# Shorter candidate lists, a fourth weight split for GpSimd, and VectorE's splits moved ahead in the choice of experts

## The chip, the cores and the metric

One core of a Trainium2 chip runs the whole program: TensorE (PE), VectorE (DVE), ScalarE (ACT), GpSimd (POOL) and the queue engine SyncE (SP), each with its own instruction stream, joined by semaphores. The metric is the device time of one execution in microseconds.

## The reference, cut to what matters

A two-layer model with a product-key mixture of experts ("PEER") in each layer, and a further block after it, on 256 tokens of width 1024, all in float32. In each layer the choice of experts is this:

```python
s1, i1 = lax.top_k(sc[:, :, 0], 16)      # sc: [256 tokens, 8 heads, 2, 128 keys]
s2, i2 = lax.top_k(sc[:, :, 1], 16)
cand = (s1[..., :, None] + s2[..., None, :])   # 16 x 16 pairs
cidx = i1[..., :, None] * 128 + i2[..., None, :]
top_s, pos = lax.top_k(cand, 16)
eidx = take_along_axis(cidx, pos)
gate = softmax(top_s)
```

After it every token's output is the sum over its 8 x 16 chosen experts of gate * gelu(x . u[e]) * v[e]. The kernel does not gather: it computes x . u for all 16384 experts, in 128 chunks of 128, and multiplies with a dense matrix of coefficients that is zero where an expert wasn't chosen.

## The kernel before, in words

**Weights.** Every weight block is a slot of 128 x 1024 float32 numbers. Slots pass through a ring of four buffers. SyncE loads slot n into `ring` once the low part of slot n-4 is made; ScalarE writes the rounded high part `ring_hi` (line 524, `split_hi`) once TensorE has used slot n-4; then VectorE or GpSimd subtracts to make the low part `ring_lo` (line 530, `split_lo`). Both engines use the same instruction with two tensors as inputs. One semaphore, `lo_ready`, counts the low parts in order of slots, so whoever makes the low part of slot n first waits until all earlier ones are there. TensorE multiplies each block in three products (lines 536 to 538: high x high, low x high, high x low), 24 matmuls a block.

**Who splits.** `POOL_SLOTS` lists the slots that GpSimd splits; VectorE takes all others, at places that are written out by hand. u0 is the first slot of the stage "expert.0" of a layer, in which TensorE multiplies 24 expert chunks while VectorE makes the choice. I call slot u0 + k **block k**. In the kernel before GpSimd splits the last query slots up to block 2, then blocks 4, 5, 6 and 14, 15, 16.

**The choice (`choose`, lines 1857 to 1938).** VectorE first finds the top 16 of the keys for each head (eight searches of 128 numbers for four rows each), then for each half t of the tokens (128 tokens, t = 0 and 1): converts the indices (L1874), builds the candidate sums (two TENSOR_TENSOR, L1882), searches the list of each head for its top 16 (`top16`, L1841 to L1854: maxima, their places, replacement, maxima, places), takes differences for the softmax (L1893, L1895), works out the two ranks of each winner from its place (L1898 to L1910), and looks up both indices (for x = 0 and 1: comparison L1915, product L1920, four sums L1926 and L1928), and scales the gates (L1934 to L1938, `picks_ready`). The sorted order of s1 and s2 means that pair (i, j) can only be among the top 16 if (i+1)(j+1) <= 16, so a list needs only some of the 256 pairs: before, 4 rows of 16 and 12 rows of 4, which is 112. Between these steps stand the calls `weights(n)`, each a split of one slot; `left` is the list of slots that is used up by the later calls.

**What follows.** TensorE transposes the picks (`turn_picks`, L922) between blocks 22 and 23; that needs `picks_ready` of both halves. ScalarE copies them out, VectorE builds one-hot matrices from them (L1977 to L1986), and TensorE multiplies these into coefficients in the next stage (L893), where another 24 expert chunks are interleaved. ScalarE's own order in expert.0 is: high part of block j+2, then the gelu of chunk j (L1332), and the softmax's exponentials (L1316) after chunks 7 and 19.

Of the kernel before, what the change touches and what calls it, by code (L numbers as in the profile page):

```python
# [16 lines left out]
ALU = mybir.AluOpType  # L17
# [25 lines left out]
PH = 8  # L43
TOPK = 16
GATE_SCALE = 2.0 ** 15
CANDS = 4 * TOPK + 4 * (TOPK - 4)
CHUNKS = NKEYS
FF = 2816
FC = FF // P
# [183 lines left out]
SLOTS, SLOT0 = plan_slots()  # L233

POOL_SLOTS = []
for _l in range(2):
    _u = SLOT0[f"expert{_l}.0"]
    POOL_SLOTS += [range(SLOT0[f"query{_l}"] + 5, _u + 3), range(_u + 4, _u + 7), range(_u + 14, _u + 17)]

# [23 lines left out]
def build(nc, a):  # L265
    with ExitStack() as ctx:
# [3 lines left out]
        def sem(name):  # L270
            return ctx.enter_context(nc.semaphore(name))
# [18 lines left out]
        rows = desk[:, :].bitcast(F16).rearrange("p (b n) -> p b n", b=3)  # L290
# [40 lines left out]
        def view(group, shape, arena=arena):  # L331

            n = int(np.prod(shape))
            at = used.get(group, 0)
            used[group] = at + n
            assert used[group] <= ARENA, group
            v = arena[:, at:at + n]
            names = "abcd"[:len(shape)]
            if len(shape) > 1:
                v = v.rearrange(f"p ({' '.join(names)}) -> p {' '.join(names)}",  # L340
                                **{x: s for x, s in zip(names[1:], shape[1:])})
            return v
# [27 lines left out]
        query = view("peer", [16, S])  # L370
# [11 lines left out]
        pair_ab = cand2.rearrange("p h n -> p (h n)")[:, 0:4 * PH * TOPK].rearrange("p (x k) -> p x k", x=4)  # L382
        pair_f = view("peer", [4 * PH * TOPK // 2]).bitcast(F16).rearrange("p (x n) -> p x n", x=4)
# [92 lines left out]
        vec = Tally(sem("vec_step"))  # L476
# [5 lines left out]
        def freed(w):  # L482
            return bank_free[w % 4], w // 4 + 1
# [1135 lines left out]
        def _(dve):  # L1619
            def step():  # L1620

                dve.wait_ge(vec.sem, vec.n)
# [234 lines left out]
            def choose(l):  # L1857
                u0 = SLOT0[f"expert{l}.0"]

                def weights(n):  # L1860

                    if any(n - 1 in r for r in POOL_SLOTS):
                        dve.wait_ge(lo_ready, n)
                    split_lo(dve, n)

                u32 = lambda v: v.bitcast(U32)
                for g in range(PH):
                    for t in range(NT):
                        dve.wait_ge(*freed(W0[f"query{l}"] + QUERY_ITEMS.index(("score", (t, g)))))
                    top16(lambda r: best[:, r // 2, 2 * g + r % 2, :], lambda r: u32(best_at[:, r // 2, 2 * g + r % 2, :]),  # L1870
                          lambda r: sub[:, g, r // 2, r % 2, :], lambda r: sub2[:, r // 2, r % 2, :], 4).then_inc(vec.sem, vec.up())
                    step()
                for t in range(NT):
                    dve.tensor_copy(best_f[:, t, :, :, :], u32(best_at[:, t, :, :]).rearrange("p (h x) r -> p x r h", x=2)).then_inc(vec.sem, vec.up())  # L1874

                    hp = best[:, t, :, :].rearrange("p (h x) k -> p h x k", x=2)
                    for lo, i0, rows, width in ((0, 0, 4, TOPK), (4 * TOPK, 4, TOPK - 4, 4)):
                        part = cand[:, :, lo:lo + rows * width].rearrange("p h (i j) -> p h i j", j=width)  # L1880
                        part_shape = [P, PH, rows, width]
                        dve.tensor_tensor(part, hp[:, :, 0, i0:i0 + rows].unsqueeze(3).to_broadcast(part_shape),  # L1882
                                          hp[:, :, 1, 0:width].unsqueeze(2).to_broadcast(part_shape), ALU.add).then_inc(vec.sem, vec.up())
                    shape = [P, PH, TOPK, TOPK]
                    step()
                    weights(u0 + (3, 13)[t])
                    left = iter(range(u0 + (7, 17)[t], u0 + (13, 24)[t]))
                    top = pair[:, t, :].rearrange("p (h k) -> p h k", k=TOPK)
                    at = pair_at.rearrange("p (h k) -> p h k", k=TOPK)
                    top16(lambda r: top[:, r, :], lambda r: u32(at[:, r, :]), lambda r: cand[:, r, 0:CANDS], lambda r: cand2[:, r, 0:CANDS], PH).then_inc(vec.sem, vec.up())  # L1890
                    step()

                    dve.tensor_copy(psum8[:, t, 1, :], top[:, :, 0]).then_inc(vec.sem, vec.up())  # L1893
                    step()
                    dve.tensor_tensor(top, top, psum8[:, t, 1, :].unsqueeze(2).to_broadcast([P, PH, TOPK]), ALU.subtract).then_inc(gate_diff_ready, 1)  # L1895

                    for y, (op, amount) in enumerate(((ALU.logical_shift_right, 4), (ALU.bitwise_and, TOPK - 1), (ALU.logical_shift_right, 2), (ALU.bitwise_and, 3))):
                        dve.tensor_scalar(u32(pair_ab[:, y, :]), u32(pair_at), amount, None, op).then_inc(vec.sem, vec.up())  # L1898
                    step()
                    weights(next(left))  # L1900
                    dve.tensor_copy(pair_f.rearrange("p x (k h) -> p x k h", h=PH), u32(pair_ab[:, :, :]).rearrange("p x (h k) -> p x k h", h=PH)).then_inc(vec.sem, vec.up())
                    step()

                    dve.scalar_tensor_tensor(pair_ab[:, 0, :], pair_f[:, 2, :], 4.0 - TOPK, pair_f[:, 0, :], ALU.add, ALU.subtract).then_inc(vec.sem, vec.up())
                    dve.tensor_tensor(pair_ab[:, 1, :], pair_f[:, 3, :], pair_f[:, 1, :], ALU.subtract).then_inc(vec.sem, vec.up())
                    step()
                    for x in range(2):
                        dve.scalar_tensor_tensor(pair_ab[:, 2 + x, :], pair_f[:, 2, :], float(TOPK), pair_ab[:, x, :], ALU.is_ge, ALU.mult).then_inc(vec.sem, vec.up())
                    step()
                    dve.tensor_tensor(pair_f[:, 0:2, :], pair_f[:, 0:2, :], pair_ab[:, 2:4, :], ALU.add).then_inc(vec.sem, vec.up())  # L1910
                    step()
                    for x in range(2):

                        shape = [P, TOPK, PH * TOPK // 4, 4]
                        dve.tensor_tensor(rank_hot.rearrange("p r (n f) -> p r n f", f=4), pair_f[:, x, :].rearrange("p (n f) -> p n f", f=4).unsqueeze(1).to_broadcast(shape),  # L1915
                                          ranks[:, :, :].unsqueeze(2).to_broadcast(shape), ALU.is_equal).then_inc(vec.sem, vec.up())
                        step()
                        weights(next(left))
                        shape = [P, TOPK, TOPK, PH]
                        dve.tensor_tensor(rank_key.rearrange("p r (k h) -> p r k h", h=PH), rank_hot.rearrange("p r (k h) -> p r k h", h=PH),  # L1920
                                          best_f[:, t, x, :, :].unsqueeze(2).to_broadcast(shape), ALU.mult).then_inc(vec.sem, vec.up())
                        step()
                        weights(next(left))

                        for n in (8, 4, 2):
                            dve.tensor_tensor(rank_key[:, 0:n, :], rank_key[:, 0:n, :], rank_key[:, n:2 * n, :], ALU.add).then_inc(vec.sem, vec.up())  # L1926
                            step()
                        dve.tensor_tensor(chosen[:, t, x, :], rank_key[:, 0, :], rank_key[:, 1, :], ALU.add).then_inc(vec.sem, vec.up())  # L1928
                        step()
                        if t or not x:  # L1930
                            weights(next(left))
                    gate = chosen[:, t, 2, :].rearrange("p (k h) -> p h k", h=PH)
                    dve.wait_ge(gate_exp_ready, NT * l + t + 1)
                    dve.tensor_reduce(psum8[:, t, 0, :], gate, AX.X, ALU.add).then_inc(vec.sem, vec.up())  # L1934
                    step()
                    dve.reciprocal(psum8[:, t, 0, :], psum8[:, t, 0, :]).then_inc(vec.sem, vec.up())
                    step()
                    dve.tensor_tensor(gate, gate, psum8[:, t, 0, :].unsqueeze(2).to_broadcast([P, PH, TOPK]), ALU.mult).then_inc(picks_ready, 1)  # L1938
# [438 lines left out]
```

## Time and profile before

| what | value |
|---|---|
| median of 3 runs | 2502.95 us (2501.2 to 2504.99) |
| profiled execution | span 2499.7 us from its first to its last instruction; no other time is listed for it |
| median less that span | 3.25 us |
| granted TensorE clock | 0.999 of full speed |
| busy in the span | PE 98%, DVE 76%, ACT 50%, POOL 5% |
| expert.0 of layer 0 | 188.3 to 263.3 us |
| expert.0 of layer 1 | 1111.2 to 1186.2 us |

The span is what the trace shows of the execution; the median is over whole executions and holds 3.25 us more. The engines' shares are averages over the program; the two stages named in the last rows are where the change lies.

### The profile page before, as it was taken

To read this page: it belongs to the slowest core of one execution; us is meant where nothing else is said; L and a number is where in the kernel's file an instruction comes from. 1 tells how busy PE (TensorE), PEld (TensorE's weight loads), DVE (VectorE), ACT (ScalarE), POOL (GpSimd) and SP (SyncE) were. 2 spreads that over 40 slices of the span, in tenths; PEclk is the share of its full clock that TensorE was granted. 3 is DMA by queue.
4 is the path that set the end of the run, shared out by engine and by line. 5 is a ranking of instruction groups with operands and counts; after the bars stand their busy time and mean duration, and the time that the engine had idled before them with its cause. 6 is when DMAs were issued, how large, how long until landed. Compare 5 with 4: busy or idle time off the path is not lost.

```text
span 2499.7 us, 48393 instructions
## 1 busy us (share of the span) xinstructions
PE 2455.1 (98%) x17776; PEld 2276.9 (91%) x17776; DVE 1900.3 (76%) x3687; ACT 1255.6 (50%) x2085; POOL 132.3 (5%) x115
## 2 busy tenths in 40 slices
PE   9999999999999999999999999999999999999999
PEld 8998998999999888999988999999889999899999
DVE  6789997666666788889996666666886767787774
ACT  6754884444444334455874444444335445556443
POOL 0042000000000000051000000000000001100000
PEclk9999999999999999999999999999999999999999
DMA  7444677666655554545676666655554555524555
GB/s 241 143 156 172 188 210 240 205 214 210 210 194 189 188 186 168 186 145 193 189 216 227 210 210 210 208 195 186 187 190 137 175 185 175 139 95 152 178 183 163
DMA packets 192136, 465.70 MB, mean 186 GB/s; under 512 B 81546, under 2 KB 83722, under 8 KB 191088
## 3 DMA queue, kind: packets, MB, share of 16 engines
q1 hardware_dynamic: 118736, 419.99, 50.6%
q0 software_dynamic: 6624, 24.28, 3.3%
q10 hardware_dynamic: 66624, 19.40, 3.2%
q8 instruction: 95, 1.56, 0.2%
q14 instruction: 57, 0.47, 0.1%
HBM read 443.02 MB, written 20.59 MB: 185 GB/s over the span
## 4 chain that ended last, share of the span: by engine, by line
PE 50%; DVE 2%; ACT 1%; issue 0%; DVEq 0%; ACTq 0%
PE acc L879 14%; PE work L536 9%; PE work L537 9%; PE work L538 9%; PE acc L536 2%; PE acc L537 1%; PE acc L538 1%; PE work L893 1%; PE work L1107 1%; DVE ring_lo L530 1%; PE work L1093 0%; PE work L1080 0%; PE work L719 0%; PE work L718 0%; PE work L717 0%
## 5 line engine op out<-in xcount | busy, mean ns | idle before, releaser
L530 DVE TENSOR_TENSOR ring_lo<-ring,ring_hi 128x1024 fp32r<-128x1024 f32 x758 | 921.3, 1219 | 429.8 <-ACT ring_hi L524 428.1
L524 ACT ACTIVATE ring_hi<-ring 128x1024 fp32r<-128x1024 f32 (+1 forms) x798 | 832.6, 1050 | 442.7 <-PE acc L879 370.1
L536 PE MATMUL work<-normed_hi,ring_hi 128*128 128x256 f32 (+1 forms) x2512 | 714.0, 284 | 17.6 <-DVE ring_lo L530 11.6
L537 PE MATMUL work<-normed_lo,ring_hi 128*128 128x256 f32 (+1 forms) x2512 | 708.5, 282 | 0.0
L538 PE MATMUL work<-normed_hi,ring_lo 128*128 128x256 f32 (+1 forms) x2512 | 706.3, 281 | 0.0
L879 PE MATMUL acc<-ring_hi,weighed 128*128 128x512 f32 x2048 | 588.4, 396 | 4.8 <-DVE weighed L2010 4.8
L536 PEld LDWEIGHTS work<-normed_hi,ring_hi 128*128 128x128 f32 x2512 | 472.7, 188 | 31.3 <-DVE ring_lo L530 13.4
L537 PEld LDWEIGHTS work<-normed_lo,ring_hi 128*128 128x128 f32 x2512 | 473.6, 189 | 7.9
L538 PEld LDWEIGHTS work<-normed_hi,ring_lo 128*128 128x128 f32 x2512 | 472.1, 188 | 0.0
L879 PEld LDWEIGHTS acc<-ring_hi,weighed 128*128 128x128 f32 x2048 | 373.8, 188 | 83.9 <-DVE weighed L2010 5.2
L536 PE MATMUL work<-arena_parts,ring_hi 128*128 128x256 f32 (+1 forms) x1184 | 336.6, 284 | 3.6 <-DVE arena L2242 2.0
L538 PE MATMUL work<-arena_parts,ring_lo 128*128 128x256 f32 (+1 forms) x1184 | 334.0, 282 | 0.0
L537 PE MATMUL work<-arena_parts,ring_hi 128*128 128x256 f32 (+1 forms) x1184 | 333.6, 282 | 0.0
L879 PE MATMUL acc<-ring_lo,weighed 128*128 128x512 f32 x1024 | 323.0, 396 | 0.0
L1332 ACT ACTIVATE arena<-work 128x256 f32 (+1 forms) x192 | 73.8, 384 | 349.7 <-PE work L538 349.7
L879 PEld LDWEIGHTS acc<-ring_lo,weighed 128*128 128x128 f32 x1024 | 192.7, 188 | 45.6
L536 PEld LDWEIGHTS work<-arena_parts,ring_hi 128*128 128x128 f32 x1184 | 223.3, 189 | 4.5 <-DVE arena L2242 2.2
L537 PEld LDWEIGHTS work<-arena_parts,ring_hi 128*128 128x128 f32 x1184 | 223.3, 189 | 0.1
L538 PEld LDWEIGHTS work<-arena_parts,ring_lo 128*128 128x128 f32 x1184 | 223.1, 188 | 0.0
L2004 DVE TENSOR_TENSOR product<-arena 128x256 f32 (+1 forms) x256 | 157.0, 613 | 2.5 <-ACT arena L1346 2.5
L536 PE MATMUL acc<-normed_hi,ring_hi 128*128 128x256 f32 x512 | 154.5, 302 | 0.0
L537 PE MATMUL acc<-normed_lo,ring_hi 128*128 128x256 f32 x512 | 143.9, 281 | 0.0
(298 smaller groups left out, 2522.1 us busy)
## 6 DMA issues: line engine op xcount, KB each, us to landing
ring<-in_u SPq DMA_DIRECT2D x256, 512.0 KB, 3.3
ring<-in_v SPq DMA_DIRECT2D x256, 512.0 KB, 3.3
ring<-in_ffn_in SPq DMA_DIRECT2D x88, 512.0 KB, 3.3
ring<-in_query SPq DMA_DIRECT2D x32, 512.0 KB, 3.3
ficients_of_later_chunks<-gate_b ACTq DMA_DIRECT2D x32, 512.0 KB, 4.6
arena<-ficients_of_later_chunks POOLq DMA_DIRECT2D x32, 512.0 KB, 4.0
ring<-in_ffn_out SPq DMA_DIRECT2D x32, 512.0 KB, 4.1
ring<-in_even_in SPq DMA_DIRECT2D x27, 512.0 KB, 3.9
```

The costliest lines, as they stand in the source:

```text
L524: act.activation(ring_hi[:, n % RING, 0:width], ring[:, n % RING, 0:width], ACT.Copy).then_inc(hi_ready, 1)
L530: eng.tensor_tensor(ring_lo[:, n % RING, 0:width], ring[:, n % RING, 0:width], ring_hi[:, n % RING, 0:width].bitcast(F32), ALU.subtract).t ...
L536: pe.matmul(out, w_hi, hi, start=start, stop=False, **more)
L537: pe.matmul(out, w_hi, lo, start=False, stop=False, **more)
L538: return pe.matmul(out, w_lo, hi, start=False, stop=stop, **more)
L879: mm = pe.matmul(acc[:, 2 * half + t, :], tokens, rows[:, m, half * 512:(half + 1) * 512], start=(e == 0 and x == 0), stop=(e == CHUNKS - ...
L893: mm = pe.matmul(work[:, w % 4, t * P:(t + 1) * P], hot_second[b][:, t // 2, :, t % 2], hot_gated[b][:, x, t // 2, :, t % 2], start=(x == ...
L1107: mm = pe.matmul(work[:, w % 4, t * P:S], v, prob2[:, u % 2, b, t:NT, :].rearrange("p t q -> p (t q)"), start=(b == 0), stop=(b == NT), sk ...
L1332: act.activation(into, work[:, w % 4, 0:S], ACT.Gelu).then_inc(bank_free[w % 4], 1)
L2004: dve.tensor_tensor(product[:, e % 2, :], hid, co, ALU.mult).then_inc(coef_read, 1)
```

## The change

Three things change, in both layers. The candidate lists have 3 rows of 16 and 13 rows of 4 pairs, which is 100 in place of 112, and the constants that turn a place into ranks follow. GpSimd splits blocks 4 to 7 and 14 to 17. VectorE's own splits are placed anew: block 3 ahead of the index conversion and candidate sums of the first half; block 8 (18 in the second half) right behind the differences; blocks 9 to 13 (19 to 23) behind the comparisons, products and the first lookup's sums. The split of block 13 was the last thing before the second search, and is now inside the second lookup of the first half.

```diff
-CANDS = 4 * TOPK + 4 * (TOPK - 4)
+WIDE = 3
+CANDS = WIDE * TOPK + 4 * (TOPK - WIDE)
...
-    POOL_SLOTS += [range(SLOT0[f"query{_l}"] + 5, _u + 3), range(_u + 4, _u + 7), range(_u + 14, _u + 17)]
+    POOL_SLOTS += [range(SLOT0[f"query{_l}"] + 5, _u + 3), range(_u + 4, _u + 8), range(_u + 14, _u + 18)]
...
                     step()
+                weights(u0 + 3)
                 for t in range(NT):
                     dve.tensor_copy(best_f[:, t, :, :, :], ...)
...
-                    for lo, i0, rows, width in ((0, 0, 4, TOPK), (4 * TOPK, 4, TOPK - 4, 4)):
+                    for lo, i0, rows, width in ((0, 0, WIDE, TOPK), (WIDE * TOPK, WIDE, TOPK - WIDE, 4)):
...
                     step()
-                    weights(u0 + (3, 13)[t])
-                    left = iter(range(u0 + (7, 17)[t], u0 + (13, 24)[t]))
+                    left = iter(range(u0 + (8, 18)[t], u0 + (14, 24)[t]))
...
                     dve.tensor_tensor(top, top, psum8[:, t, 1, :]..., ALU.subtract).then_inc(gate_diff_ready, 1)
+                    weights(next(left))
 
                     for y, (op, amount) in enumerate(...):
                         dve.tensor_scalar(u32(pair_ab[:, y, :]), u32(pair_at), amount, None, op).then_inc(vec.sem, vec.up())
                     step()
-                    weights(next(left))
...
-                        if t or not x:
+                        if not x:
                             weights(next(left))
```

GpSimd's stream first: `ring_lo` rows are its splits, a row that waits for `lo_ready` waits for VectorE's split of the slot before. This is layer 0 before, from its first query slot to its first load of coefficients:

```order
L530 ISA
L530 TENSOR_TENSOR ring_lo<-ring,ring_hi 128x1024 [waits hi_ready,lo_ready]
L530 TENSOR_TENSOR ring_lo<-ring,ring_hi 128x1024 [waits hi_ready] x13
L530 TENSOR_TENSOR ring_lo<-ring,ring_hi 128x1024 [waits hi_ready,lo_ready]
L530 TENSOR_TENSOR ring_lo<-ring,ring_hi 128x1024 [waits hi_ready] x2
L530 TENSOR_TENSOR ring_lo<-ring,ring_hi 128x1024 [waits hi_ready,lo_ready]
L530 TENSOR_TENSOR ring_lo<-ring,ring_hi 128x1024 [waits hi_ready] x2
```

And the same place in the changed kernel, whose line numbers are higher by one:

```order
L531 ISA
L531 TENSOR_TENSOR ring_lo<-ring,ring_hi 128x1024 [waits hi_ready,lo_ready]
L531 TENSOR_TENSOR ring_lo<-ring,ring_hi 128x1024 [waits hi_ready] x13
L531 TENSOR_TENSOR ring_lo<-ring,ring_hi 128x1024 [waits hi_ready,lo_ready]
L531 TENSOR_TENSOR ring_lo<-ring,ring_hi 128x1024 [waits hi_ready] x3
L531 TENSOR_TENSOR ring_lo<-ring,ring_hi 128x1024 [waits hi_ready,lo_ready]
L531 TENSOR_TENSOR ring_lo<-ring,ring_hi 128x1024 [waits hi_ready] x3
```

Each of the two later groups has four splits in place of three. VectorE's stream before, at the start of the first half: the conversion, the candidate sums, the split of block 3 and the search.

```order
L1874 CAST arena<-arena 128x256
L1882 TENSOR_TENSOR arena<-arena 128x8x64
L1882 TENSOR_TENSOR arena<-arena 128x8x48
L530 TENSOR_TENSOR ring_lo<-ring,ring_hi 128x1024
L1841 MAX arena<-arena 128x8 x8
```

In the changed kernel the split of block 3 stands first, and it is what releases GpSimd for blocks 4 to 7:

```order
L531 TENSOR_TENSOR ring_lo<-ring,ring_hi 128x1024
L1876 CAST arena<-arena 128x256
L1884 TENSOR_TENSOR arena<-arena 128x8x48
L1884 TENSOR_TENSOR arena<-arena 128x8x52
L1842 MAX arena<-arena 128x8 x8
```

VectorE's stream before, from the last sums of the first half's second lookup to the second search:

```order
L1926 TENSOR_TENSOR arena<-arena 128x256
L1928 TENSOR_TENSOR arena<-arena 128x128
L1934 TENSOR_REDUCE arena<-arena 128x8
L1936 RECIPROCAL arena<-arena 128x8
L1938 TENSOR_TENSOR arena<-arena 128x8x16
L1874 CAST arena<-arena 128x256
L1882 TENSOR_TENSOR arena<-arena 128x8x64
L1882 TENSOR_TENSOR arena<-arena 128x8x48
L530 TENSOR_TENSOR ring_lo<-ring,ring_hi 128x1024
L1841 MAX arena<-arena 128x8 x8
```

In the changed kernel, the same stretch from block 13's split on:

```order
L531 TENSOR_TENSOR ring_lo<-ring,ring_hi 128x1024
L1927 TENSOR_TENSOR arena<-arena 128x1024
L1927 TENSOR_TENSOR arena<-arena 128x512
L1927 TENSOR_TENSOR arena<-arena 128x256
L1929 TENSOR_TENSOR arena<-arena 128x128
L1935 TENSOR_REDUCE arena<-arena 128x8
L1937 RECIPROCAL arena<-arena 128x8
L1939 TENSOR_TENSOR arena<-arena 128x8x16
L1876 CAST arena<-arena 128x256
L1884 TENSOR_TENSOR arena<-arena 128x8x48
L1884 TENSOR_TENSOR arena<-arena 128x8x52
L1842 MAX arena<-arena 128x8 x8
```

The split that releases GpSimd for blocks 14 to 17 has moved from just ahead of the search to ten other instructions earlier.

## Rows read from the trace of the kernel before

**Rows 1.** The page: the span, and busy time (share of the span) by engine.
```profile
span 2499.7 us, 48393 instructions
PE 2455.1 (98%) x17776; PEld 2276.9 (91%) x17776; DVE 1900.3 (76%) x3687; ACT 1255.6 (50%) x2085; POOL 132.3 (5%) x115
```

**Rows 2.** Waits in expert.0, layer 0 then 1: us in total, times, longest.
```profile
PE work L536 <- DVE ring_lo L530: 5.3, 4, 1.5
...
PE work L536 <- DVE ring_lo L530: 5.4, 4, 1.5
```

**Rows 3.** TensorE's timeline: start us, us, what, xcount [idle before <- releaser].
```profile
198.11 0.39 PE L536 MATMUL work<-normed_hi,ring_hi 128*128 128x256 f32 x1 [1.09 <-DVE ring_lo L530]
...
214.12 0.39 PE L536 MATMUL work<-normed_hi,ring_hi 128*128 128x256 f32 x1 [1.48 <-DVE ring_lo L530]
...
229.76 0.38 PE L536 MATMUL work<-normed_hi,ring_hi 128*128 128x256 f32 x1 [1.24 <-DVE ring_lo L530]
...
245.77 0.39 PE L536 MATMUL work<-normed_hi,ring_hi 128*128 128x256 f32 x1 [1.47 <-DVE ring_lo L530]
```

**Rows 4.** ScalarE's timeline: high part of block 5, gelu of chunks 4 and 5.
```profile
197.33 1.05 ACT L524 ACTIVATE ring_hi<-ring 128x1024 fp32r<-128x1024 f32 x1
...
204.07 0.39 ACT L1332 ACTIVATE gate_b<-work 128x256 f32<-128x256 f32 x1 [1.50 <-PE work L538]
...
206.89 0.38 ACT L1332 ACTIVATE gate_b<-work 128x256 f32<-128x256 f32 x1 [1.50 <-PE work L538]
```

**Rows 5.** VectorE over both halves: stretch and its length, busy; then its waits.
```profile
195.30:260.10 64.80, 62.77 (x204) 1.00 0.51 179
...
DVE ring_lo L530 <- ACT ring_hi L524: 0.3, 1, 0.3
```

**Rows 6.** Timeline, last instruction of the choice and TensorE's transposes of the picks.
```profile
259.74 0.42 DVE L1938 TENSOR_TENSOR arena<-arena 128x128 f32<-128x128 f32 x1
...
260.01 0.82 PE L922 MATMUL work<-const,arena 128*128 128x128 f32 x6
```

**Rows 7.** VectorE's timeline in the first half.
```profile
195.32 0.41 DVE L1874 CAST arena<-arena 128x256 f16<-128x256 uint32 x1
195.63 1.17 DVE L1882 TENSOR_TENSOR arena<-arena 128x512 f32<-128x512 f32 x2
196.83 1.23 DVE L530 TENSOR_TENSOR ring_lo<-ring,ring_hi 128x1024 fp32r<-128x1024 f32 x1
197.97 1.51 DVE L1841 MAX8 arena<-arena 128x8 f32<-128x112 f32 x8
...
199.59 0.27 DVE L1845 FIND_INDEX8 arena<-arena 128x8 uint32<-128x112 f32 x1
...
207.18 0.17 DVE L1893 COPY arena<-arena 128x8 f32<-128x8 f32 x1
...
208.26 1.23 DVE L530 TENSOR_TENSOR ring_lo<-ring,ring_hi 128x1024 fp32r<-128x1024 f32 x1
...
224.14 1.47 DVE L1926 TENSOR_TENSOR arena<-arena 128x1024 f16<-128x1024 f16 x3
...
225.98 0.43 DVE L1934 TENSOR_REDUCE arena<-arena 128x8 f32<-128x128 f32 x1
...
226.68 0.41 DVE L1938 TENSOR_TENSOR arena<-arena 128x128 f32<-128x128 f32 x1
```

**Rows 8.** Groups by form, lists of 128 and 112 numbers: busy us, mean ns.
```profile
L1854 DVE FIND_INDEX8 arena<-arena 128x8 uint32<-128x128 f32 x2 | 0.5, 285 | 0.0
...
L1854 DVE FIND_INDEX8 arena<-arena 128x8 uint32<-128x112 f32 x1 | 0.3, 268 | 0.0
```

**Rows 9.** GpSimd's splits: durations (ns min/median/max) of all 40, and its timeline.
```profile
L530 POOL TENSOR_TENSOR ring_lo<-ring,ring_hi x40: 2374/2397/2417, 147.5 to 1157.5; 128x1024 fp32r<-128x1024 f32 x40
...
198.13 7.11 POOL L530 TENSOR_TENSOR ring_lo<-ring,ring_hi 128x1024 fp32r<-128x1024 f32 x3 [5.68 <-DVE ring_lo L530]
229.79 7.12 POOL L530 TENSOR_TENSOR ring_lo<-ring,ring_hi 128x1024 fp32r<-128x1024 f32 x3 [24.54 <-DVE ring_lo L530]
```

More of the change, by code:

```diff
@@ L1899, in choose @@
                     step()
-                    weights(next(left))
                     dve.tensor_copy(pair_f.rearrange("p x (k h) -> p x k h", h=PH), u32(pair_ab[:, :, :]).rearrange("p x (h k) -> p x k h", h=PH)).then_inc(vec.sem, vec.up())
                     step()
-                    dve.scalar_tensor_tensor(pair_ab[:, 0, :], pair_f[:, 2, :], 4.0 - TOPK, pair_f[:, 0, :], ALU.add, ALU.subtract).then_inc(vec.sem, vec.up())
+                    dve.scalar_tensor_tensor(pair_ab[:, 0, :], pair_f[:, 2, :], WIDE - 4.0 * WIDE, pair_f[:, 0, :], ALU.add, ALU.subtract).then_inc(vec.sem, vec.up())
                     dve.tensor_tensor(pair_ab[:, 1, :], pair_f[:, 3, :], pair_f[:, 1, :], ALU.subtract).then_inc(vec.sem, vec.up())
@@ L1907, in choose @@
                     for x in range(2):
-                        dve.scalar_tensor_tensor(pair_ab[:, 2 + x, :], pair_f[:, 2, :], float(TOPK), pair_ab[:, x, :], ALU.is_ge, ALU.mult).then_inc(vec.sem, vec.up())
+                        dve.scalar_tensor_tensor(pair_ab[:, 2 + x, :], pair_f[:, 2, :], 4.0 * WIDE, pair_ab[:, x, :], ALU.is_ge, ALU.mult).then_inc(vec.sem, vec.up())
                     step()
```

## The prediction

> **What bounds the kernel now.** I read the page first: TensorE is busy 98% of the 2499.7 us, so time can only come from, or go to, the places where it waits [rows 1]. The waits of expert.0 name one cause, `ring_lo` from VectorE: 5.3 us in four waits in layer 0 and 5.4 us in four in layer 1 [rows 2]. The timeline places them: blocks 3, 8, 13 and 18 [rows 3]. TensorE takes 206.89 - 204.07 = 2.82 us a block [rows 4]; 24 blocks are 67.7 us, the stage lasts 75.0 and the transposes take some 0.6, so about 6.5 us a layer are really lost (the profile models the end of a matmul late, so it shows 5.3).
>
> VectorE makes most of those splits between the steps of the choice, and it is full: from 195.3 to 260.1 it waits once, 0.3 us [rows 5]. Its chain also sets the end of the stage. Its last instruction, L1938, runs 259.74 to 260.16, and TensorE starts the transposes of the picks at 260.01, first half first [rows 6]. So TensorE arrives there just when VectorE is done: **two chains end together**. Taking away TensorE's waits alone gives nothing; the stage ends earlier only by as much as VectorE's chain gets shorter, up to 6.5 us a layer.
>
> **The change, part by part, if VectorE and GpSimd run freely beside each other.**
> - Two splits a layer go to GpSimd (blocks 7 and 17). On VectorE a split costs the distance to the next instruction, 197.97 - 196.83 = 1.14 us [rows 7]: 2 x 1.14 = 2.28 us.
> - A list is 12 numbers shorter. A place search of 128 numbers took 285 ns and one of 112 took 268: 1.06 ns a number [rows 8], 12.8 ns an instruction. A half has 5 groups of 8 search instructions (two of maxima, two of places, one of replacement; the small value loads between them don't change): 40 x 12.8 = 0.51 us. The candidate sums have 96 numbers fewer, 0.10 us. Two halves: 1.22 us. The constants that turn a place into ranks cost nothing: same instructions, same sizes.
> - The 0.3 us wait of rows 5 was for ScalarE's high part of block 22. With an earlier TensorE it goes, against which VectorE may wait a little at blocks 8 and 10, where it is now earlier than ScalarE. I take 0.2 net.
> - Together 3.7 us of VectorE a layer. TensorE: block 3's wait goes, since its split stands 1.5 us earlier (195.32 instead of 196.83 [rows 7]); blocks 8 and 13 come in time. The other 2.8 us of its 6.5 it will still wait, at block 19 or for the picks. So it is VectorE's 3.7 us, not TensorE's 6.5, that the stage gains.
> - GpSimd's fourth split in each group is hidden by TensorE's pace: a split takes 2.40 us [rows 9], less than 2.82 a block, and ScalarE's high parts come one a block.
>
> Freely beside each other this gives 2502.95 - 2 x 3.7 = 2495.5.
>
> **What the new places bring together.** All 40 splits of GpSimd in the profile take 2.374 to 2.417 us, and every one lies beside a search or an idle VectorE; in expert.0 the groups start at 198.13 and 229.79, right behind VectorE's split of blocks 3 and 13, and end within the searches [rows 7, 9]. A search instruction reads one tensor. Beside GpSimd it costs nothing: 0.27 us at 199.59, as long as one without [rows 7, 8]. But a split on either engine reads two. There is **no row in which a two-tensor instruction of VectorE lies beside a split of GpSimd**, and the change makes many:
> - First half. Block 4 can start 0.07 us behind VectorE's block 3 (198.13 against 196.83 + 1.23 [rows 7, 9]), so at 196.6; the candidate sums would start at 195.32 + 1.14 + 0.31 = 196.8.
> - Between the halves. Block 13's split now stands inside the second lookup and releases blocks 14 to 17. Then come sums L1926 and L1928 (224.14 to 225.98: 1.8 us), the reduction and reciprocal (0.7 us, one tensor) and L1938 [rows 7], the conversion and candidate sums (1.5 us): 4.4 us, most of it two-tensor, ahead of the second search.
>
> The cost is bounded by nothing (above: 3.7 us gained), and by each engine waiting for the other's whole instruction. In that case, worked out on the first layer:
> - Candidate sums wait from 196.8 to 199.0 (2.2 us); if GpSimd's block 5 follows at once, whose high part is there at 198.4 [rows 4], to 201.4 (4.6 us).
> - Between the halves at least two splits get in: one at the reduction, so L1938 waits 2.4 - 0.7 = 1.7 us, the next ahead of the candidate sums, 2.2 us. At most VectorE stands behind three to four splits, 8.8 us: GpSimd's rows come merged in threes at 7.11 us, so its splits follow with no gap when the high parts are there [rows 9].
> - Sum: 6.1 to 13.4 us a layer, middle 9.8.
>
> VectorE's chain is then longer than before by 9.8 - 3.7 = 6.1 us a layer, TensorE waits for blocks 8 or 9 and for 18 and 19, and the picks come 6 us late. What stands behind the picks shifts by the same: VectorE builds one-hots from them without a break, and TensorE has no slack in 98% of the span. Two layers: +12.2, ends +4.8 and +19.4.
>
> The Trainium skill speaks against the change here: "SBUF — State Buffer", section "Who interferes with whom", says that a VectorE instruction with two inputs in SBUF and a GpSimd instruction that reads SBUF contend for a shared read interface, and that the second to start is blocked until the first has finished. By it the sum is the second one, 2515; by rows 9 alone, which show no such pair, both ends stay open.
>
> **Which end I take.** No row decides. The break-even does part of it: 3.7 us a layer is one and a half GpSimd splits, and at least four of the eight in a layer fall where VectorE wants two tensors. If a third of their 9.6 us is waited for, the gain is gone. Of all shares of waiting between none and all, most lie on the losing side. So I forecast **waiting: 2502.95 + 12 = 2515**, its own range 2505 to 2523.
>
> **Rivals.**
> - Free overlap: 2495.5. For it: nothing in the profile shows a cost of running both. Against it: nothing shows that pair. Chance 0.20. This is the one on the other side; it decides from less than 3.7 us of waiting a layer.
> - Short waiting: VectorE's three sums L1926 follow each other without a gap (1.47 us merged [rows 7]), so GpSimd may find a gap only at the reduction, and at block 4 it might come behind the candidate sums. Then 2 to 6 us a layer: -1.7 to +2.3, 2500 to 2508. Chance 0.22, two thirds of it within 0.2%.
> - GpSimd's own lateness: if its block 17 is not there when block 18 is due, VectorE stands (it waits for `lo_ready`). GpSimd needs 4 x 2.40 = 9.6 us and, at one high part per 2.82 us, spans some 11 us against a search of 8.7 (207.18 - 197.97 - 0.51 [rows 7]). That by itself costs little, since block 17 starts over 2 us before the search ends; only a delay by VectorE's instructions makes it matter. It lies inside the forecast.
> - The forecast, 6 to 13 us of waiting: 0.58.
>
> **The numbers.** A measurement of this kernel can tell about 0.2% (5 us) from no change. Slower by more: 0.58 less the part of it that just touches +4.8 (0.04), plus 0.06 of the short waiting, 0.60. Within 0.2%: 0.15 + 0.04, 0.19. Faster: 0.20 and 0.01, 0.21. The range must reach the free case, since that alone holds 2 in 10: 2495 to 2523.
>
> **What the new profile would show.** Right: VectorE's candidate sums of the first half begin late, by 2 us or more, with no semaphore as a cause, or last over 2 us; the same at L1939 (the old L1938) and the second candidate sums; splits longer than 2.42 us on GpSimd and 1.23 on VectorE; TensorE waits at blocks 8 or 9 and 18, 19; picks later than 260.2. Wrong: the candidate sums take 1.1 us together and start at once, the picks are done near 256.4, and TensorE waits only at block 19 and ahead of the transposes. A search must be shorter by 0.5 us in either case: that is a check on the 1.2 us of the lists. What would make the forecast wrong is a free pair; what would make it wrong in size is how the two engines take turns, on which I took the middle.

## The result, and the profile after

The changed kernel takes 2513.7 us (median of 4 runs, 2511.28 to 2518.85) against 2503.11 us for the kernel before, measured beside it (4 runs, 2501.2 to 2504.99): ratio 1.0048, interval 1.0036 to 1.006. It is slower by 10.6 us. The profiled execution has a span of 2509.7 us and a time of its own of 2511.63.

The page's first lines, which answer to [rows 1]:

```profile
span 2509.7 us, 48391 instructions
PE 2460.5 (98%) x17776; PEld 2281.7 (91%) x17776; DVE 1909.6 (76%) x3683; ACT 1255.8 (50%) x2085; POOL 144.4 (6%) x119
```

VectorE has two splits a layer less, 4 x 1.14 = 4.6 us, and shorter lists, and yet 9.3 us more busy time. That is the first sign: a wait for the other engine is counted as work. The rows to look at are VectorE's in the first half of layer 0 (timeline: start us, us, instruction, count, idle before):

```profile
195.18 1.23 DVE L531 TENSOR_TENSOR ring_lo<-ring,ring_hi 128x1024 fp32r<-128x1024 f32 x1
196.32 0.39 DVE L1876 CAST arena<-arena 128x256 f16<-128x256 uint32 x1
196.63 5.47 DVE L1884 TENSOR_TENSOR arena<-arena 128x384 f32<-128x384 f32 x2
202.13 1.41 DVE L1842 MAX8 arena<-arena 128x8 f32<-128x100 f32 x8
...
210.85 0.17 DVE L1894 COPY arena<-arena 128x8 f32<-128x8 f32 x1
```

and between the halves:

```profile
226.67 1.23 DVE L531 TENSOR_TENSOR ring_lo<-ring,ring_hi 128x1024 fp32r<-128x1024 f32 x1
227.81 1.47 DVE L1927 TENSOR_TENSOR arena<-arena 128x1024 f16<-128x1024 f16 x3
...
229.64 0.41 DVE L1935 TENSOR_REDUCE arena<-arena 128x8 f32<-128x128 f32 x1
230.09 0.20 DVE L1937 RECIPROCAL arena<-arena 128x8 f32<-128x8 f32 x1
230.33 1.86 DVE L1939 TENSOR_TENSOR arena<-arena 128x128 f32<-128x128 f32 x1
...
232.31 3.26 DVE L1884 TENSOR_TENSOR arena<-arena 128x384 f32<-128x384 f32 x2
```

GpSimd's splits over the same time:

```profile
196.48 10.24 POOL L531 TENSOR_TENSOR ring_lo<-ring,ring_hi 128x1024 fp32r<-128x1024 f32 x4 [4.19 <-DVE ring_lo L531]
229.50 2.41 POOL L531 TENSOR_TENSOR ring_lo<-ring,ring_hi 128x1024 fp32r<-128x1024 f32 x1 [22.78 <-ACT ring_hi L525]
232.24 2.41 POOL L531 TENSOR_TENSOR ring_lo<-ring,ring_hi 128x1024 fp32r<-128x1024 f32 x1 [0.33 <-ACT ring_hi L525]
235.04 5.21 POOL L531 TENSOR_TENSOR ring_lo<-ring,ring_hi 128x1024 fp32r<-128x1024 f32 x2 [0.39 <-ACT ring_hi L525]
```

Lay the two side by side. The split of 229.50 ends at 231.91; L1939, started at 230.33, ends 0.28 us after that, at 232.19. The split of 232.24 ends at 234.65; the two sums of L1884 end at 235.57. The reduction and the reciprocal in the same split's shadow keep their usual length [rows 7]. The timeline merges the sums of L1884; the groups by form take them apart, for 196.5 to 202.3 us (busy us, mean ns):

```profile
L1884 DVE TENSOR_TENSOR arena<-arena 128x416 f32<-128x416 f32 x1 | 2.8, 2782 | 0.0
L1884 DVE TENSOR_TENSOR arena<-arena 128x384 f32<-128x384 f32 x1 | 2.8, 2761 | 0.0
```

Each stood behind one split of 2.4 us, with 0.0 us of idle time and no releaser shown. GpSimd pays a little too: its four splits take 10.24 us here and 9.47 in a kernel in which no two-tensor instruction lies beside them (experiment 3).

TensorE waits at blocks 8 and 9, 18 and 19 and for the picks (timeline of layer 0; the first four rows answer to [rows 3], the last to [rows 6]):

```profile
212.54 0.39 PE L537 MATMUL work<-normed_hi,ring_hi 128*128 128x256 f32 x1 [1.49 <-DVE ring_lo L531]
...
217.78 0.39 PE L537 MATMUL work<-normed_hi,ring_hi 128*128 128x256 f32 x1 [2.16 <-DVE ring_lo L531]
...
246.02 0.39 PE L537 MATMUL work<-normed_hi,ring_hi 128*128 128x256 f32 x1 [1.23 <-DVE ring_lo L531]
...
251.28 0.38 PE L537 MATMUL work<-normed_hi,ring_hi 128*128 128x256 f32 x1 [2.17 <-DVE ring_lo L531]
...
264.42 0.52 PE L923 MATMUL work<-const,arena 128*128 128x128 f32 x3 [1.24 <-DVE arena L1939]
```

**Where the 10.0 us of the span went.** I measure the choice from its first instruction to the end of its last one. Before, 195.32 to 260.16: 64.84 us [rows 6, 7]. After, 195.18 to 264.27 (L1939 starts at 263.88 and takes 0.39): 69.09, and in layer 1 by the same reckoning 69.16 against 64.86. That is +4.25 and +4.30. The remaining 1.5 us lie between the two choices. Windows over the same 5792 matmuls, before and after (stretch and length; busy us of PE, PEld, DVE, ACT, POOL; granted clock; DMA share; GB/s), first the kernel before:

```profile
264.00:1111.20 847.20, 838.54 (x5792) 761.86 (x5791) 649.16 (x1190) 413.06 (x665) 40.56 (x31) 1.00 0.60 196
...
356.00:376.00 20.00, 17.53 (x156) 15.88 (x156) 18.25 (x34) 14.92 (x35) 0.00 (x0) 1.00 0.73 213
```

and the changed kernel:

```profile
268.00:1116.70 848.70, 840.14 (x5792) 763.48 (x5792) 649.40 (x1190) 413.13 (x664) 40.57 (x31) 1.00 0.61 196
...
360.00:380.00 20.00, 17.52 (x149) 15.76 (x149) 18.25 (x34) 13.82 (x34) 0.00 (x0) 0.91 0.77 215
```

The second pair is the place: the same busy time, seven matmuls fewer, and a granted clock of 0.91 where it was 1.00. A share of 0.91 over 20 us is some 3.5 us at the lower of TensorE's two levels (1.2 in place of 2.4 GHz), and costs half of that. The profile of experiment 6, whose granted clock between the choices is 1.00 as in the kernel before, has 858.4 us from the end of one choice to the start of the next (262.05 to 1120.49); the kernel before has 858.2 (260.16 to 1118.34), the changed kernel 859.6 (264.27 to 1123.87). So 8.5 us are what the two choices have become longer, and 1.5 us a dip of TensorE's clock 100 us later.

### The profile page after: what moved, and what is told of

Its sections match the earlier page's. It is cut to its first block, busy times and chain, and to the rows that moved or that the text cites. A ratio compares the mean times of both kernels' runs of the same rounds, so it can differ in the third digit from the quotient of the medians.

```text
span 2509.7 us, 48391 instructions
## 1 busy us (share of the span) xinstructions
PE 2460.5 (98%) x17776; PEld 2281.7 (91%) x17776; DVE 1909.6 (76%) x3683; ACT 1255.8 (50%) x2085; POOL 144.4 (6%) x119
## 4 chain that ended last, share of the span: by engine, by line
PE 50%; DVE 2%; ACT 1%; issue 0%; DVEq 0%; ACTq 0%
PE acc L880 14%; PE work L537 9%; PE work L538 9%; PE work L539 9%; PE acc L537 2%; PE acc L538 1%; PE acc L539 1%; PE work L894 1%; PE work L1108 1%; DVE ring_lo L531 1%; PE work L1094 0%; PE work L1081 0%; PE work L720 0%; PE work L719 0%; PE work L718 0%
## 5 line engine op out<-in xcount | busy, mean ns | idle before, releaser
L531 DVE TENSOR_TENSOR ring_lo<-ring,ring_hi 128x1024 fp32r<-128x1024 f32 (+1 forms) x754 | 916.6, 1219 | 430.6 <-ACT ring_hi L525 428.9
```

The costliest lines, as they stand in the source:

```text
L531: eng.tensor_tensor(ring_lo[:, n % RING, 0:width], ring[:, n % RING, 0:width], ring_hi[:, n % RING, 0:width].bitcast(F32), ALU.subtract).t ...
```

## The experiments

Times are compared with the kernel before, measured beside each version. "Chain" is the length of the choice from its first instruction to the end of its last, in layer 0 where nothing else is said: 64.84 us before and 69.09 after. Dots in a diff stand for lines left out.

### 1. The lists alone

The kernel before, with lists of 100 and their constants, nothing else.

```diff
-CANDS = 4 * TOPK + 4 * (TOPK - 4)
+WIDE = 3
+CANDS = WIDE * TOPK + 4 * (TOPK - WIDE)
...
```

> The kernel before with the lists of 100 pairs alone; GpSimd's three splits and all places as before. Theory of waiting (a two-tensor instruction of VectorE and a split on GpSimd exclude each other): nothing lies side by side here, so the candidate sums take 1.1 us together, each search 8.7 us in place of 9.2, the picks come 1.2 us earlier a layer, and the time falls by 2.4 us to about 2500.7. Rival, the list's shape (rows of 48 and 52 sums make the two TENSOR_TENSOR slow by themselves): the sums take 3 to 5.5 us as in the changed kernel, and the time rises by 6 us or more.

Measured: 2500.43 us (11 runs) against 2502.84, ratio 0.9988 (0.9979 to 0.9997). VectorE's timeline has the candidate sums at their usual length:

```profile
195.37 1.06 DVE L1883 TENSOR_TENSOR arena<-arena 128x384 f32<-128x384 f32 x2
```

Chain 63.63: 1.2 us shorter, as the prediction's 1.22, and 2.4 us of time for two layers. The lists are the part of the change that pays.

### 2. Blocks 3 and 13 split at the searches again

The changed kernel, with four splits on GpSimd and short lists, but released where the kernel before releases them.

```diff
-                weights(u0 + 3)
                 for t in range(NT):
...
                     step()
-                    left = iter(range(u0 + (8, 18)[t], u0 + (14, 24)[t]))
+                    weights(u0 + (3, 13)[t])
+                    left = iter(range(u0 + (8, 18)[t], u0 + (13, 24)[t]))
...
-                        weights(next(left))
+                        if t or not x:
+                            weights(next(left))
```

> The changed kernel (lists of 100, four splits on GpSimd) with the splits of block 3 and block 13 put back directly ahead of the searches, so that GpSimd starts only there. Theory of waiting: candidate sums 1.1 us in both halves, L1939 0.4 us, picks 2.5 to 3.7 us earlier a layer than in the kernel before (the fourth split may still reach past the search and hold the differences by up to 0.8 us a half); 2496 to 2498. Rival, the fourth split on GpSimd is itself what costs: no better than the kernel before, 2503 or more. Rival, TensorE's waits at blocks 8, 9, 18, 19 come from the new places of VectorE's later splits: these stay, since those places stay, and the time is near 2510.

Measured: 2502.95 us (11 runs), ratio 1.0002 (0.9993 to 1.0011). The long instructions are gone, and with them the 10 us; but the time stays 5 to 7 us above what I expected. VectorE's timeline:

```profile
195.60 1.06 DVE L1883 TENSOR_TENSOR arena<-arena 128x384 f32<-128x384 f32 x2
...
206.55 1.20 DVE L1894 COPY arena<-arena 128x8 f32<-128x8 f32 x1
...
226.80 1.05 DVE L1883 TENSOR_TENSOR arena<-arena 128x384 f32<-128x384 f32 x2
...
237.75 1.23 DVE L1894 COPY arena<-arena 128x8 f32<-128x8 f32 x1
```

GpSimd's:

```profile
205.31 2.41 POOL L531 TENSOR_TENSOR ring_lo<-ring,ring_hi 128x1024 fp32r<-128x1024 f32 x1 [0.17 <-ACT ring_hi L525]
...
236.53 2.41 POOL L531 TENSOR_TENSOR ring_lo<-ring,ring_hi 128x1024 fp32r<-128x1024 f32 x1 [0.23 <-ACT ring_hi L525]
```

The copy of eight numbers per row, 0.17 us otherwise [rows 7], ends at 207.75, right behind the end of the fourth split at 207.72. The search is over before that split is, because ScalarE's high parts come one a block. So the fourth split saves VectorE 1.14 us and costs it 1.03 of waiting. Chain 63.86, 1.0 us shorter. That would be 2.0 us of time for two layers, and the time shows none, for two reasons that the profile holds. Between the choices the granted clock is 0.93 from 355 to 380 us, where the kernel before has 1.00. And in layer 1 the chain is 65.35, 0.5 us longer than before. There the granted clock is 0.57 from 1153 to 1157 us, right behind a wait of 2.80 us of TensorE, and the high parts come late. VectorE's rows, the second search of layer 1 just ended:

```profile
1161.73 0.17 DVE L1894 COPY arena<-arena 128x8 f32<-128x8 f32 x1
1161.93 0.29 DVE L1896 TENSOR_TENSOR arena<-arena 128x128 f32<-128x128 f32 x1
1164.86 1.23 DVE L531 TENSOR_TENSOR ring_lo<-ring,ring_hi 128x1024 fp32r<-128x1024 f32 x1 [2.63 <-ACT ring_hi L525]
```

The copy runs in its usual 0.17 us ahead of GpSimd's fourth split (1162.03), but the split of block 18 stands for ScalarE, and starts 1.6 us later after the choice's first instruction than in layer 0 (239.39). By these rows a dip of TensorE's clock inside a choice can reach VectorE through ScalarE.

### 3. GpSimd held until the sums are done

The changed kernel with all its early places; a new semaphore lets GpSimd start only once the candidate sums are built.

```diff
...
                 pool.wait_ge(lo_ready, slots[0])
+                if x % 3:
+                    pool.wait_ge(search_go, 2 * (x // 3) + x % 3)
...
                     step()
+                    dve.engine_nop().then_inc(search_go, 1)
```

> The changed kernel with all VectorE splits at their new places, but GpSimd's blocks 4 to 7 and 14 to 17 begin only once the candidate sums are done (one more semaphore, raised by an empty instruction of VectorE). Theory of waiting: sums 1.1 us, L1939 0.4 us, all the loss gone; picks 2.5 to 3.7 us earlier a layer than in the kernel before, TensorE's wait at block 3 gone; 2496 to 2498, about as the kernel with blocks 3 and 13 at the searches. Rival, that VectorE's early splits cost by their place: the time stays at 2510 to 2514.

Measured: 2501.66 us (11 runs), ratio 0.9996 (0.9987 to 1.0005). The sums take 1.05 us in both halves, so VectorE's early split as such costs nothing: it is GpSimd's start that does. The copy is held again, most in the second half. VectorE's row, then GpSimd's:

```profile
237.92 2.33 DVE L1898 COPY arena<-arena 128x8 f32<-128x8 f32 x1
```

```profile
198.49 9.47 POOL L532 TENSOR_TENSOR ring_lo<-ring,ring_hi 128x1024 fp32r<-128x1024 f32 x4 [5.56 <-DVEq L1891]
...
237.83 2.39 POOL L532 TENSOR_TENSOR ring_lo<-ring,ring_hi 128x1024 fp32r<-128x1024 f32 x1 [1.45 <-ACT ring_hi L526]
```

The chain is 64.6 us, 0.2 shorter than before.

I had expected 2496 to 2498 here and in experiment 2, and missed both. For experiment 2 I had allowed the fourth split to reach past the search by up to 0.8 us a half, and here by nothing; it costs 1.0 us a half there, and 0.8 and 2.2 us here. I had also thought that only the difference behind the copy could be held, but experiment 9 shows that this changes little. What is left beyond that, the profiles' dips of the clock can account for, at some 1.5 us each; no run here is without them.

### 4. Three splits, at the early places

The changed kernel with GpSimd's groups cut back to blocks 4 to 6 and 14 to 16; blocks 7 and 17 go to VectorE. It asks whether the fourth split or the early release makes the loss.

```diff
-... range(_u + 4, _u + 8), range(_u + 14, _u + 18)]
+... range(_u + 4, _u + 7), range(_u + 14, _u + 17)]
...
-                    left = iter(range(u0 + (8, 18)[t], u0 + (14, 24)[t]))
+                    left = iter(range(u0 + (7, 17)[t], u0 + (14, 24)[t]))
...
```

> The changed kernel with three splits on GpSimd in each group (blocks 7 and 17 back on VectorE), the early places kept. Theory of waiting: the first sums still wait 4.4 us and L1939 or the second sums still wait, VectorE has 2.3 us more to do a layer, so the time is at or above the changed kernel's, 2512 to 2518. Rival, the fourth split is what costs: back to 2500 to 2503.

Measured: 2518.48 us (5 runs, up to 2522.28), ratio 1.0064 (1.0051 to 1.0078), the slowest of all, and just above the 2512 to 2518 that I expected. VectorE's timeline:

```profile
196.62 5.50 DVE L1884 TENSOR_TENSOR arena<-arena 128x384 f32<-128x384 f32 x2
...
231.46 2.17 DVE L1939 TENSOR_TENSOR arena<-arena 128x128 f32<-128x128 f32 x1
...
233.75 5.47 DVE L1884 TENSOR_TENSOR arena<-arena 128x384 f32<-128x384 f32 x2
```

Now the second sums stand behind two splits as well, 4.4 + 1.8 + 4.4 = 10.6 us a layer. With 1.2 us for the lists the chain should be 9.4 us longer; it is 74.1, +9.3. Two layers of that are 18.6 us; the median is 15.6 above the kernel before and the profiled execution, the slowest of the five, 20.7 in its span, with a mean granted clock of 0.993. The theory that four splits overtax GpSimd falls: fewer splits made it worse.

### 5. Which pairs of instructions wait

The kernel before with one GpSimd instruction added beside the candidate sums: a sum of two tensors and a memset in the two halves of layer 0, a copy in the first half of layer 1, nothing in the second. An empty instruction of VectorE, just ahead of the conversion, releases each. Their results are used by nobody, and nothing is left out.

```diff
...
+                    if turn == 1:
+                        pool.tensor_tensor(pair_out[:, 0:768], const[:, 0:768], const[:, 0:768], ALU.add)...
+                    elif turn == 2:
+                        pool.memset(pair_out[:, 0:768], 0.0)...
+                    elif turn == 3:
+                        pool.tensor_copy(pair_out[:, 0:768], const[:, 0:768])...
...
```

> The disputed cost by itself: the kernel before, with one extra GpSimd instruction released just ahead of the index conversion and candidate sums, its result unused. First half of layer 0: a GpSimd TENSOR_TENSOR of 768 numbers (two tensors read, some 1.8 us by 2.40 us for 1024). Second half of layer 0: a memset of 768 (nothing read, some 0.7 us). First half of layer 1: a copy of 768 (one tensor read). Second half of layer 1: nothing. Theory of waiting: beside the TENSOR_TENSOR the first sum of 512 lasts 0.70 us plus what is left of GpSimd's instruction, 2.2 to 2.4 us; with nothing beside it 0.70. If it is the reading that excludes, the copy costs too, for its own length less 0.2 us, and the memset nothing (0.70); if any GpSimd instruction excludes, the memset costs about 0.5 us. Rival, no exclusion at all and the long sums of the changed kernel have another cause: 0.70 us in all four.

Measured: 2506.7 us in one run against 2502.83. GpSimd's timeline:

```profile
195.52 1.64 POOL L622 TENSOR_TENSOR hot_first<-const 128x768 f32<-128x768 f32 x1 [2.98 <-DVEq L1887]
...
228.55 0.91 POOL L624 MEMSET hot_first<- 128x768 f32 x1 [21.85 <-DVEq L1887]
...
1121.20 1.01 POOL L626 COPY hot_first<-const 128x768 f32<-128x768 f32 x1 [2.95 <-DVEq L1887]
```

VectorE's groups by form, for the first half and then, under the dots, for the second (busy us, mean ns):

```profile
L1896 DVE TENSOR_TENSOR arena<-arena 128x512 f32<-128x512 f32 x1 | 2.0, 1967 | 0.0
...
L1896 DVE TENSOR_TENSOR arena<-arena 128x512 f32<-128x512 f32 x1 | 0.7, 694 | 0.0
```

Beside the two-tensor sum VectorE's sum takes 1967 ns, beside the memset 694; beside the copy the pair of sums takes 1.80 us in place of 1.16. I had expected 2.2 to 2.4 us beside GpSimd's sum; that sum took 1.64 us, less than the 1.8 I had worked out, so less of it was left to wait for. One pair of each kind was measured. What counts on GpSimd's side, by these three, is that it reads. This is what the Trainium skill states in "SBUF — State Buffer", section "Who interferes with whom": a VectorE instruction with two inputs in SBUF contends with a GpSimd instruction that reads there, and not with one that only writes. These rows agree with it.

### 6. Only block 13 moved back

The changed kernel with block 13 split at the second search again. It prices the early block 3 alone.

```diff
-                    left = iter(range(u0 + (8, 18)[t], u0 + (14, 24)[t]))
+                    if t:
+                        weights(u0 + 13)
+                    left = iter(range(u0 + (8, 18)[t], u0 + (13, 24)[t]))
...
```

> The changed kernel with only block 13's split put back directly ahead of the second search; block 3 stays early. Of the 8.1 us of long VectorE instructions a layer, the 4.4 at the first sums stay and the 3.7 at L1939 and the second sums go; in exchange the COPY behind the second search waits about 1.1 us as in the kernel with both splits at the searches. Theory of waiting: picks 2.6 us earlier a layer than in the changed kernel, 2508 to 2509. Rival, the waits don't add up because TensorE's rhythm absorbs them: 2512 or more, or 2505 or less.

Measured: 2505.94 us (11 runs) against 2502.83, ratio 1.0016 (1.0007 to 1.0025). VectorE's timeline:

```profile
196.69 5.48 DVE L1884 TENSOR_TENSOR arena<-arena 128x384 f32<-128x384 f32 x2
...
229.89 1.06 DVE L1884 TENSOR_TENSOR arena<-arena 128x384 f32<-128x384 f32 x2
```

The first sums are held as before, the second are free, and the copy of the second half takes 1.19 us. Chain 66.8 in both layers, +2.0. That is 2.3 us a layer shorter than in the changed kernel, where I had expected 2.6. I had expected a time of 2508 to 2509, and it is 2 us below that. Of the 10.6 us of the change, 3.1 remain, but the times alone mislead about the shares: the profile of this version, taken in its fastest execution, has no dip of the clock between the choices (1.00 from 355 to 380 us), nor one from 1285 to 1305 us where the kernel before has 0.91. By the chains of layer 0, block 13's early place costs 69.09 - 66.81 = 2.28 us, and block 3's 66.81 - 63.86 = 2.95, the larger part.

### 7. Three splits, held until the sums are done

Experiment 3 with three splits in each group: what is left when neither the sums nor the copy can meet GpSimd.

```diff
-... range(_u + 4, _u + 8), range(_u + 14, _u + 18)]
+... range(_u + 4, _u + 7), range(_u + 14, _u + 17)]
...
```

> Lists of 100, three splits on GpSimd held back until the candidate sums are done, VectorE's splits at their new early places. Nothing two-tensor and no COPY lies beside GpSimd any more (three splits of 2.37 us fit in a search of 8.7). Theory of waiting: VectorE's chain is as short as with the lists alone, less about 0 to 0.3 us a layer for the extra instruction and semaphore: 2500 to 2501. Rival, the early places of VectorE's splits help TensorE by themselves: 2498 or less. Rival, they hurt: 2503 or more.

Measured: 2499.32 us (11 runs), ratio 0.9988 (0.9979 to 0.9997). Sums 1.05 us, copy 0.17 in both halves, chain 63.6. It ties with the lists alone, so the early places of VectorE's splits are worth nothing measurable; these two are the best versions, and both beat the kernel before and the changed one. I had expected 2500 to 2501.

### 8. The index conversion as a filler

Experiment 2, with the conversion of the indices moved behind the search. If a one-input conversion doesn't wait for GpSimd, it fills the fourth split's tail.

```diff
-                    dve.tensor_copy(best_f[:, t, :, :, :], ...)      # ahead of the sums
...
+                    dve.tensor_copy(best_f[:, t, :, :, :], ...)      # ahead of the copy
                     dve.tensor_copy(psum8[:, t, 1, :], top[:, :, 0])
```

> The kernel e2 (lists of 100, four GpSimd splits, blocks 3 and 13 split at the searches), with the index conversion (CAST, 0.4 us, 0.3 us to the next instruction) moved from ahead of the candidate sums to behind the search, where the COPY waits 1.0 us for GpSimd's fourth split. Theory of waiting: the conversion reads one tensor and runs at once beside GpSimd, so it fills that wait; VectorE's chain is 0.3 us shorter a half, 1.2 us in all: 0.8 to 1.6 us below e2, about 2501.5. Rival: the conversion is held too, as the COPY is; no change from e2.

Measured: 2501.89 us (11 runs) against 2502.67, ratio 0.9996 (0.9987 to 1.0005). VectorE's timeline:

```profile
206.34 1.43 DVE L1893 CAST arena<-arena 128x256 f16<-128x256 uint32 x1
207.70 0.15 DVE L1894 COPY arena<-arena 128x8 f32<-128x8 f32 x1
```

The conversion, 0.41 us otherwise [rows 7], is held for 1.0 us itself. My premise fell, although the time is 1.1 us below experiment 2's, as it had forecast: that agreement is luck. The chain is 63.25, 0.6 us shorter than in experiment 2. It isn't the conversion that gains this. VectorE starts the first half's difference 12.5 us after the choice's first instruction in both, and what the second half saves ahead of its sums is lost again behind its search. The gain lies in the gaps ahead of VectorE's own splits, 0.35 us from the difference to the split of block 8 in experiment 2 and 0.21 here; in all, experiment 2's profile shows 0.5 us of waiting for ScalarE's high parts in this choice, this one 0.2. Why ScalarE's parts cost less here was not tried.

### 9. A reduction in place of the copy

Experiment 2, with the copy of the maxima replaced by a reduction that gives the same numbers.

```diff
-                    dve.tensor_copy(psum8[:, t, 1, :], top[:, :, 0])
+                    dve.tensor_reduce(psum8[:, t, 1, :], top, AX.X, ALU.max)
```

> The kernel e2 with the COPY of each head's largest value behind the search replaced by a TENSOR_REDUCE (maximum of the sorted 16, the same value). If what holds the COPY for 1.0 us is that this kind of instruction excludes GpSimd's split although it reads one tensor, the TENSOR_REDUCE takes 0.4 us or less at once and the TENSOR_TENSOR behind it is held instead, 0.8 us or so; the chain is as long as before. Rival, the COPY is held by something it shares with any instruction at that place (a dependency on the search's end): the TENSOR_REDUCE lasts 1.2 us or more.

Measured: 2502.4 us in one run. VectorE's timeline:

```profile
206.52 0.29 DVE L1894 TENSOR_REDUCE arena<-arena 128x8 f32<-128x128 f32 x1
206.84 0.99 DVE L1896 TENSOR_TENSOR arena<-arena 128x128 f32<-128x128 f32 x1
```

The reduction runs at once inside GpSimd's fourth split (205.28 to 207.69), and the two-tensor difference behind it is held until that split is over. The chain is 63.7 us, as long as experiment 2's to within 0.2: sparing the copy its wait gains nothing, since the difference waits in its place. So copy and conversion wait and the reduction doesn't, though all three read one tensor. The same section of "SBUF — State Buffer" in the Trainium skill has this distinction: copies and casts can enter modes that take the shared pair of ports, a reduction on this chip never does. The rows agree on who waits; no run here shows which mode a copy of eight numbers ran in.

## Why the prediction came out as it did

I forecast 2515.0 with waiting as the mechanism; 2513.7 was measured.

- **Two chains end together.** Right. The picks come at 264.27 instead of 260.16, and the stages behind shift by it. In the other direction, chains shorter by 1.2 us a layer (experiments 1 and 7) gave 2.4 to 3.5 us of time; in experiment 2 one shorter by 1.0 in layer 0, but longer by 0.5 in layer 1, gave none, with the lower clock named there.
- **What the lists save.** Right: forecast 1.22 us a layer, 1.2 measured in experiment 1. The search runs 202.13 to 210.85, 8.72 us, against 9.21 before: the 0.5 us named as the check.
- **VectorE waits for GpSimd's whole instruction.** Right, and shown from three sides: the rows of the changed kernel, their disappearance when only GpSimd's start moves (experiment 3), and the isolated pairs (experiment 5).
- **How much waiting.** The term that was mis-sized. I had 6.1 to 13.4 us a layer and took 9.8. Measured: 5.47 - 1.06 = 4.4 at the first sums, 1.86 - 0.41 = 1.45 at L1939, 3.26 - 1.06 = 2.2 at the second sums, 8.1 in all. At the first sums the higher case held (4.6 forecast). Between the halves it was 3.65 us, even below my low end of 1.7 + 2.2 = 3.9, and the 8.8 at the top was far off: ScalarE's high parts let GpSimd go only at 229.50, 232.24 and 235.04, so the sums of L1927 were over and the next split came too late for the second sum. Experiment 4, where VectorE ran later against ScalarE, shows the other case.
- **The sum.** 8.1 - 2.28 - 1.22 and the 0.3 us wait of [rows 5] give +4.3 us a layer, where I had +6.1; measured are +4.25 and +4.30. Two layers: 8.5 us instead of 12.2. The time came out nearer to the forecast than that, because 1.5 us of the span were lost at a lower granted clock, for which the forecast had no term. Part of the agreement is luck.
- **Where TensorE waits.** Blocks 8, 9, 18 and 19, as named. GpSimd's own splits stretch only by 0.77 us over four; VectorE's stay at 1.23.
- **"GpSimd's fourth split in each group is hidden by TensorE's pace".** Wrong, but without weight in this kernel, where the group starts early enough. It is hidden from TensorE and not from VectorE: released at the search, its tail outlasts the search and holds the copy or the difference behind it. So the free case's 3.7 us a layer, 2495.5, can't be had by moving the release alone. Of the 2.28 us that I counted for two splits nothing is left in experiment 2: its chain is 1.0 us shorter, where the lists alone gave 1.2.

**Rivals.** Free overlap falls with experiments 2, 3 and 5. Short waiting falls by size: 8.1 us against its 2 to 6; its picture of the second half (few gaps between the sums) was nearer the truth than my middle. GpSimd's own lateness falls with experiment 4, and VectorE shows no wait for it in the changed kernel's choice.

**Open.** What makes TensorE's clock dip at 360 to 380 us in the changed kernel, and near that place in the profiles of all experiments but the sixth (0.93 from 355 to 380 us, in experiment 4 0.91 from 380 to 400), and not in the profile before, is not settled. Executions of one kernel differ in it: the kernel before has a mean clock of 0.999 in most, and 0.998 in those of 2504.5 us or more. A gain or loss of 1 or 2 us of time is therefore read from the chains and not from the medians. In the choice of layer 0 a window row places a dip (0.89, then 0.68) in the 8 us from 216 on, right behind the longest wait, at 217.78; VectorE waits for nobody in that choice, so it cost nothing there, other than in layer 1 of experiment 2. But experiment 1 has the dip near 370 with shorter waits, and experiment 6 has the same long wait (2.2 us) and no dip near 370. Whether the changed kernel's waits cause its own was not tried.

## What to carry to other kernels

These rules are drawn from the pairs measured here. Before an operation is moved to a second vector engine, list what stands beside it on the first one: the price of the helper is not its own time but that of every two-tensor instruction, copy and conversion that falls into its instructions, each waiting up to one whole instruction of the helper. Put the helper's work under searches and reductions, start it there and not when its data happen to be ready, and size it so that it ends before they do. When VectorE's busy time rises though it has less to do, compare each instruction's duration with the same shape elsewhere; there is no idle time to find.

## What the hardware showed that I had not expected

- A copy of 8 numbers per row (0.17 us) and a conversion of 256 (0.41 us), each with one input, were held for 1.0 us beside GpSimd's split, the copy once for 2.2 us. TENSOR_REDUCE (0.29 us in experiment 9), RECIPROCAL (0.20), MAX8, FIND_INDEX8 and MATCH_REPLACE8 were not.
- The two engines alternate instruction by instruction: between GpSimd's back-to-back splits VectorE got in exactly one sum, 2761 and 2782 ns for each in place of some 0.5.
- TensorE, 98% busy, shows a stretch or more of some 3.5 us at the lower clock in every profile of this case, in varying places: 0.91 over 1285 to 1305 us in the kernel before, 0.83 over 1300 to 1310 in the changed one.
